# Expert weights laid out by adjacent rows: 16 KB and 8 KB per partition, transposes of every other column, 2 MB transfers

## What is computed

```python
logits = (xt @ w_router + b_router).astype(jnp.float32)
top_val, top_idx = lax.top_k(logits, TOP_K)          # 4 of 32 experts
gates = jax.nn.softmax(top_val, axis=-1)
...
def expert_block(args):
    x_blk, e = args
    hid = x_blk @ w_gate_up[e] + b_gate_up[e]        # w_gate_up[e]: 1024 x 2048
    gate, up = hid[:, :D_FF], hid[:, D_FF:]
    gate = jnp.minimum(gate, SWIGLU_LIMIT)
    up = jnp.clip(up, -SWIGLU_LIMIT, SWIGLU_LIMIT)
    glu = gate * jax.nn.sigmoid(SWIGLU_ALPHA * gate)
    return ((up + 1.0) * glu) @ w_down[e] + b_down[e]  # w_down[e]: 1024 x 1024
```

## Time and profile before

| | us |
|---|---|
| median of three runs | 1595.6 (1593.41 to 1595.63) |
| the profiled execution | 1589.94 |
| its span, first to last instruction | 1588.1 |
| TensorE busy in the span | 1402.4 |
| VectorE, ScalarE, GpSimd busy | 608.3, 302.9, 329.8 |
| the expert loop, 507.2 to 1546.0 | 1038.8 |

### The profile page before, as it was taken

How to read it: one execution, slowest core, us unless ns; L and a number is a source line. 1 busy time by engine, 2 the same in 40 slices (tenths; PEclk the granted TensorE clock), 3 DMA queues, 4 the chain that set the end, 5 groups by cost and what they waited for, 6 DMA issues and landing times.

```text
span 1588.1 us, 33877 instructions
## 1 busy us (share of the span) xinstructions
PE 1402.4 (88%) x13302; PEld 664.2 (42%) x13303; DVE 608.3 (38%) x1529; ACT 302.9 (19%) x563; POOL 329.8 (21%) x355
## 2 busy tenths in 40 slices
PE   6997989879748998899998989989999998899982
PEld 2444555545413443444343444433444344334441
DVE  2688777653353222223222322223323223222231
ACT  3113323131201111112111111211212122111222
POOL 5001101020011222222222131223222222212222
PEclk9999999979868999899999999999999999999996
DMA  9212000130267999999999999999999999999995
GB/s 308 63 61 73 1 27 1 40 122 17 80 245 253 351 370 398 372 400 404 342 387 373 411 386 312 393 366 402 408 406 407 396 409 404 401 408 404 410 377 143
DMA packets 110262, 457.76 MB, mean 288 GB/s; under 512 B 15140, under 2 KB 36132, under 8 KB 77430
## 3 DMA queue, kind: packets, MB, share of 16 engines
q1 hardware_dynamic: 86566, 427.88, 68.3%
q0 software_dynamic: 20592, 27.68, 7.5%
q10 hardware_dynamic: 3072, 1.76, 0.4%
HBM read 439.05 MB, written 18.22 MB: 288 GB/s over the span
## 4 chain that ended last, share of the span: by engine, by line
PE 63%; DMA 13%; DVE 11%; issue 5%; ACT 3%; POOL 2%; SPq 1%; POOLq 1%; ACTq 0%; DVEq 0%
PE bank L1838 23%; PE bank L1880 18%; DMA spare<-in_gdn_dt_bias_dram 6%; PE bank L1526 5%; DMA ring<-in_w_gate_up_dram 4%; PE bank L1700 3%; PE bank L1906 3%; PE bank L1810 2%; DMA acc_rows<-rows,idx 2%; DVE dslots L962 2%; POOL acc_rows L535 1%; ACT rows L852 1%; PE bank L1591 1%; DVE qkbuf L986 1%; PE bank L1521 1%
## 5 line engine op out<-in xcount | busy, mean ns | idle before, releaser
L1838 PE MATMUL bank<-ring,wq 128*32 128x512 f32 x5184 | 580.6, 602 | 18.3 <-DMA ring<-in_w_gate_up_dram 16.1
L1838 PEld LDWEIGHTS bank<-ring,wq 128*32 128x32 f32 x5184 | 163.0, 111 | 385.0 <-issue 384.5
L1880 PE MATMUL bank<-dslots,intra 128*32 128x256 f32 x5056 | 306.8, 390 | 3.3 <-issue 2.3
L1880 PEld LDWEIGHTS bank<-dslots,intra 128*32 128x32 f32 x5056 | 170.6, 113 | 121.8 <-issue 36.0
L529 POOL DMA_INDIRECT wq<-xn_rows,idx x88 | 87.5, 994 | 537.6 <-PE bank L1810 477.2
L535 POOL DMA_INDIRECT acc_rows<-rows,idx x83 | 134.7, 1623 | 305.6 <-ACT rows L852 270.5
L845 ACT ACTIVATE wq<-bank 128x512 f32<-128x512 f32 x128 | 66.1, 602 | 600.6 <-PE bank L1838 600.6
L1326 DVE COPY idx<-idx 128x4 int32<-128x4 int32 x99 | 16.9, 170 | 380.1 <-POOLq L589 195.0
L1526 PE MATMUL bank<-hbuf,ring 128*128 128x512 f32 x320 | 146.5, 597 | 0.0
L1407 DVE TENSOR_TENSOR intra<-bank,small 128x256 f32<-128x256 f32 x128 | 45.4, 418 | 256.4 <-PE bank L1906 246.8
L962 DVE SCALAR_TENSOR_TENSOR dslots<-dslots,small 128x512 f32<-128x512 f32 x120 | 92.2, 768 | 3.4 <-DVE rows L1082 0.6
(11 more groups left out here) (279 smaller groups left out, 1051.7 us busy)
## 6 DMA issues: line engine op xcount, KB each, us to landing
ring<-in_w_gate_up_dram SPq DMA_DIRECT2D x256, 1024.0 KB
dslots<-in_w_down_dram SPq DMA_DIRECT2D x124, 1024.0 KB
ring<-in_w_in_dram SPq DMA_DIRECT2D x12, 1024.0 KB
ring<-in_w_out_dram SPq DMA_DIRECT2D x4, 1024.0 KB
ring<-in_w_down_dram SPq DMA_DIRECT2D x4, 1024.0 KB
rows<-in_x_dram SPq DMA_DIRECT2D x4, 512.0 KB, 7.3
hbuf<-in_x_dram SPq DMA_DIRECT2D x4, 512.0 KB, 5.2
xn_rows<-convbuf POOLq DMA_DIRECT2D x4, 512.0 KB, 4.7
```

The source lines that it names most:

```text
L1838: ins = M(bank[g][GROUP * j:GROUP * (j + 1), :], xT[:, g, c % 2, (c // 2) * GROUP:(c // 2 + 1) * GROUP], w[:, :, j * QD:(j + 1) * QD], sta ...
L1880: ins = M(b[GROUP * j:GROUP * (j + 1), col:col + QD], actT[:, g, c % 2, (c // 2) * GROUP:(c // 2 + 1) * GROUP], w[:, cc, j * QD:(j + 1) * QD],
```

## The change

The rows of an expert's weights are dealt to the partitions in another way. Partition p takes two adjacent rows, 2p and 2p+1, of each block of 256: 16 KB in one piece for gate/up and 8 KB in one piece for down. Two gate/up slots are filled by one transfer of 2 MB, four a visit, issued when both are used; down stays at four transfers of 1 MB. The contraction index of a chunk is then every other column of the quarter, so the transposes of tokens, hidden values and biases read every other column. The down weights of the last expert, which lie in the ring, get semaphores of their own.

```diff
-            def gate_up(i, c):
+            def gate_up(i, q):
                 e = i % E
-                sp.dma_start(view(ring, c * SLOT, SLOT), w_gate_up[0, e, c * P:(c + 1) * P, :]).then_inc(
-                    slot_in[c], 16)
+                sp.dma_start(view(ring, 2 * q * SLOT, 2 * SLOT),
+                             w_gate_up[0, e, 2 * q * P:(2 * q + 2) * P, :].rearrange("(p c) n -> p (c n)", c=2)
+                             ).then_inc(slot_in[2 * q], 16)
             def down(i, u):
                 e = i % E
                 sp.dma_start(view(dslots, u * SLOT, 2, D),
-                             w_down[0, e, 2 * u * P:(2 * u + 2) * P, :].rearrange("(c p) n -> p c n", p=P)
+                             w_down[0, e, 2 * u * P:(2 * u + 2) * P, :].rearrange("(p c) n -> p c n", c=2)
                              ).then_inc(slot_in[8 + u], 16)
...
             with sp.Fori(2, m + 2) as i:
-                for c in range(KC):
-                    sp.wait_ge(gu_used, (i - 1) * KC + c + 1)
-                    gate_up(i, c)
+                for q in range(KC // 2):
+                    sp.wait_ge(gu_used, (i - 1) * KC + 2 * q + 2)
+                    gate_up(i, q)
...
+            def every_other(v, start, first):
+                return v[:, start:start + QD].rearrange("p (n two) -> p n two", two=2)[:, :, first]
...
-                        ins = TR(b[:, c:c + P], xg[:, g, hh * P:(hh + 1) * P], ident)
+                        ins = TR(b[:, c:c + P], every_other(xg[:, g, :], 0, hh), ident)
...
-                w = view(ring, c * SLOT, 2, D)
+                w = view(ring, 2 * (c // 2) * SLOT, 2, 2, D)[:, c % 2, :, :]
...
                 for c0 in range(0, KC, 2):
                     pe.wait_ge(slot_in[c0], i * 16 + 48)
-                    pe.wait_ge(slot_in[c0 + 1], i * 16 + 48)
...
                     if last:
-                        pe.wait_ge(slot_in[u], i * 16 + 64)
+                        pe.wait_ge(last_in[u], 16)
...
                         ins = TR(bank[6 + g // 2][:, c:c + P],
-                                 hid[:, g, half * QD + hh * P:half * QD + (hh + 1) * P], ident)
+                                 every_other(hid[:, g, :], half * QD, hh), ident)
```

More of the change, by code:

```diff
@@ L273, in block_kernel @@
         half_read, router_ready = sem("half_read"), sem("router_ready")
+        last_in = [sem(f"last_in{u}") for u in range(4)]
         class Own:
@@ L379, in _ @@
                 sp.dma_start(x2[:, t, :], x2d[t * P:(t + 1) * P, :]).then_inc(xres_in[t], 16)
-            for c in range(KC):
-                if c == 4:
+            for q in range(KC // 2):
+                if q == 2:
                     sp.wait_ge(op_done, T)
-                if c == 6:
+                if q == 3:
                     sp.wait_ge(xn_ready, T)
-                gate_up(0, c)
+                gate_up(0, q)
             for u in range(4):
@@ L391, in _ @@
             m = visits_less_two(sp)
-            for c in range(KC):
-                sp.wait_ge(gu_used, c + 1)
-                gate_up(1, c)
+            for q in range(KC // 2):
+                sp.wait_ge(gu_used, 2 * q + 2)
+                gate_up(1, q)
             with sp.Fori(2, m + 2) as i:
-                for c in range(KC):
-                    sp.wait_ge(gu_used, (i - 1) * KC + c + 1)
-                    gate_up(i, c)
+                for q in range(KC // 2):
+                    sp.wait_ge(gu_used, (i - 1) * KC + 2 * q + 2)
+                    gate_up(i, q)
                 for u in range(4):
@@ L405, in _ @@
                 sp.dma_start(view(ring, u * SLOT, 2, D),
-                             w_down[0, E - 1, 2 * u * P:(2 * u + 2) * P, :].rearrange("(c p) n -> p c n", p=P)
-                             ).then_inc(slot_in[u], 16)
+                             w_down[0, E - 1, 2 * u * P:(2 * u + 2) * P, :].rearrange("(p c) n -> p c n", c=2)
+                             ).then_inc(last_in[u], 16)
             sp.wait_ge(scattered, m * (16 * GROUPS) + 32 * GROUPS)
@@ L1480, in bias_turn @@
                 for j in range(2 * KC):
-                    ins = TR(view(bank[5], 0, 2 * KC, E)[:, j, :], bgu_rows[:, j * P:(j + 1) * P], ident[0:E, 0:E])
+                    ins = TR(view(bank[5], 0, 2 * KC, E)[:, j, :], every_other(bgu_rows, j // 2 * QD, j % 2),
+                             ident[0:E, 0:E])
                 ins.then_inc(bias_turned, 1)
```

## The result

The changed kernel takes 1703.3 us (median of four runs, 1701.0 to 1707.2) against 1594.5 us of the kernel before on the same chip (1591.1 to 1595.6): 1.069 times the time, 95% interval 1.066 to 1.072. It is slower by some 109 us; the forecast was 1747 us, in a range of 1615 to 1785.

A forecast was written before the change was run, and what follows sets the result against it. Scatter, `numbers` and token transposes were taken to bound visits with two groups, late weights from about 1070 us. 1589.9 + 152 (scatter waits) - 18 (weight waits) + 18 (clock) = 1742, so 1747 us for the runs; range 1615 to 1785.

The forecast's parts named there:

- What bounds the kernel: Expert loop: the scatter bounds visits with two groups, 45 us of waits; from about 1070 us late weights bound, 16.1 us.
- The price of a turn: DMA engines beside gate/up: a scattered row waits for one whole weight packet, so a turn grows from 0.403 to 0.70 us.
- The length of the wait: TensorE's waits for `numbers` at the token transposes, line 1810: 197 us in place of 45, so +152 us.
- all turns would lie beside a packet of 16 KB: Every scatter turn was counted 0.30 us longer: 5.4, 7.5 or 9.6 us with two, three or four groups.
- the visits with three groups only, at half strength: Three groups, scatter of three: part of the scatter finds queue 1 empty, so a wait of 3 us, not 5.8.
- the 5 us taken off the last visit: Last visit: down packets lie beside its scatter, 8 KB in place of 4 KB, so 5 us less wait.
- The rival of the half price: Scatters: queue 1 may run empty between pairs, so half the turns are short, half of 152, 1670 us; chance 0.14.
- The transposes: Transposes reading every other float, 24 a visit: taken as nothing; bound double, 3.3 us a visit, 101 us; rival's chance 0.03.
- The clock: TensorE behind long waits: a lower clock costs about 2.2 us a visit, in 8 more visits, +18 us.
- Weights: TensorE's waits for weights go as visits get slower, -18 us; the transfer itself gains between 0 and 11 us.
- small packets do not wait for 16 KB: Rival, DMA engines: if they switch by bytes, the scatter turn stays 0.40 us and the time is 1585 us; chance 0.10.
- rows are cut: Rival, gate/up transfers: 16 KB may go as two packets of 8 KB, 1588 to 1600 us, taken at 1594; chance 0.07.

## Why the prediction was right, and where its sizes were off

*What bounds the kernel.* Right. The chain of scatter, `numbers` and token transposes ended the visits with two groups, and became longer in all of them. Taking its wait away made the kernel before faster by 1.9% and the changed one by 8.7% (1.068 to 0.975).

*The price of a turn.* Right. 0.70 us was worked out from the packets of 4 and 8 KB, 0.71 was measured. With a scatter of two groups 18.2 us from POOL to `numbers` against 18.7 forecast.

*The length of the wait.* The mechanism was right, the size too large: 152 us against 199 (197 and the two ahead of the loop). The failed step is that all turns would lie beside a packet of 16 KB. With four groups I had 28.0 us and a wait of 17.1, measured are 25.5 and 14.52. The queues of 1094:1096, at the start of that scatter, show why:

```profile
q0 software_dynamic: 144, 0.13, 58.8%
q1 hardware_dynamic: 10, 0.16, 40.0%
```

The first group, 128 rows, goes through while queue 1 is all but empty, as the slower visits let the weights be in time; 8 turns of 0.30 us are 2.4 of the 2.5 us that are missing. I had used this for the visits with three groups only, at half strength, and there it was worth all: they have 0.4 us of wait where 20 were forecast. By kind of visit, measured against forecast: nine with two groups and a scatter of two 66 us against 72, six with a scatter of three 55 against 76 (71 with the 5 us taken off the last visit), two with a scatter of four 29 against 34. So the size was nearly right where queue 1 has work during the whole scatter: in visit 1048.5 it is never empty, and by the packets of the trace 179 of the 256 rows move beside packets of 16 KB. In visit 898.9 the queues of 903:907 move 318 packets of queue 0 beside 97 of queue 1:

```profile
q1 hardware_dynamic: 97, 0.84, 60.7%
q0 software_dynamic: 318, 0.26, 46.9%
```

The rival of the half price had this reason in it, the queue running empty between pairs; it holds for the first group of a scatter, not for half of the turns.

*The transposes.* I took nothing and kept double as the bound, and named more than 1.09 us for eight at full clock as a sign against it. That sign came: they cost 13 us in the loop. The weight loads of these transposes (line 1911, before 1906) take 209 ns at the median in place of 140; eight transposes take 1.23 us in place of 1.09. The rows, first after, then before:

```profile
L1911 PEld LDWEIGHTS bank<-consts,wq x512: 194/209/226, 509.1 to 1660.0; 128*128 128x128 f32 x171
```

```profile
L1906 PEld LDWEIGHTS bank<-consts,wq x512: 137/140/231, 501.7 to 1545.4; 128*128 128x128 f32 x171
```

And eight transposes without a wait ahead of them, in visit 898.9:

```profile
920.26 1.23 PE L1816 MATMUL bank<-consts,wq 128*128 128x128 f32 x8
```

The Trainium skill's rule on 16-byte lines (SBUF — State Buffer, Door 1) would have a step of two floats at full rate. The rows differ from it: the load is longer by half, and the two pairs of runs with and without the step are 4 and 11 us apart.

*The clock.* 18 us forecast, about 14 measured, by the busy time of lines 1885 and 1816. All the token transposes behind a long wait take 1.98 us.

*Weights.* Their waits went, as forecast. What the transfer gains could not be seen in the changed kernel; it is seen once the scatter is off the path: 411 to 414 GB/s in the windows 900:1000, 1100:1200 and 1300:1400, against 402 to 406 in the kernel before with that edit, and the changed kernel ends 0.6 points ahead, with its slower transposes counted in.

*The rivals.* That small packets do not wait for 16 KB is refuted by the turn of 0.71 us. That rows are cut is refuted by the 3.67 MB in 256 packets: in pieces of 8 KB they would be 448. A late release by pairs and a doubled transfer cost nothing, as assumed (0.999).

*Open.* The loop begins at 514.5 us in the changed kernel's profile and at 507.2 before. In the profile of the run with plain transposes, which has the same transfers, it begins at 509.1. Some of it is a lower granted clock in the first part (0.81 in 336:380 against 0.84 in 333:375), which I can't tie to the change.

## What to carry to other kernels

Large weight packets and small latency-bound packets share the DMA engines turn by turn. So before packets are made larger, look for a chain that waits for small transfers beside them, and count its turns: rows per engine times the extra time of one large packet. Take that wait off the path first (here by a copy of 16 bytes a partition); then the larger packets pay a little (0.975 against 0.981), and in the other order they cost 7%.

## What the runs showed of the hardware

- Two queues with work take turns on a DMA engine packet by packet: 444 packets to 440 with 8 KB beside 1 KB, 256 to 260 with 16 KB.
- A packet's time is a straight line from 4 to 16 KB as far as the turns show it (0.245, 0.40 and 0.71 us with a scattered row of 1 KB beside it), and 32 KB with 1.34 us lies near it (1.29). The packets' own durations in the traces, at the median, are 0.159, 0.309, 0.611 and 1.213 us, and 0.101 for the scattered row.
- At equal bytes the rate in the loop rises with the packet: 396 to 398 GB/s with 4 KB for all weights, 402 to 406 with 8 KB for gate/up and 4 KB for down, 408 to 411 with 8 KB for both, 411 to 414 with 16 and 8 KB, each in the windows 900:1000, 1100:1200 and 1300:1400 and with gathers and scatters beside them.
- A weight load of 128 x 128 float32 with a step of two elements takes 209 ns in place of 140, and of this 0.14 us come through for eight transposes in a row.
